# Rotation by DMA exchange, attention's back steps in one group per round, group norm by groups, two tiles in turns behind norms

## The chip, the core and the metric

The kernel runs on one core of one Trainium2 chip: a single program on its five engines, TensorE (PE), VectorE (DVE), ScalarE (ACT), GpSimd (POOL) and SyncE (SP), which work through instruction streams of their own and meet at semaphores. The metric is the device time of one execution in microseconds; the time given is the median of the timed executions.

## What is computed

One layer of a first block on x (512 tokens, width 1024) and a context (256 tokens): a gated feed-forward net (width 2816) on both, a mixing layer (a Fourier part and a two-directional state-space scan with a group norm), and a second feed-forward net. Then two layers of a second block with four branches of 8 heads of 64 channels: A, attention with forget gates; B, attention over 256 chosen tokens; D, attention in a window of 128; C, retention. What the change touches, shortened:

```
def rms_norm(x, g):                         # ahead of and behind every sublayer
    y = x32 * lax.rsqrt(jnp.mean(x32 * x32, axis=-1, keepdims=True) + EPS)
    return (y * g.astype(jnp.float32)).astype(x.dtype)
...
    y = y.reshape(b, L, SSD_WIDTH).astype(x.dtype) * jax.nn.silu(z)
    y = rms_norm(y.reshape(b, L, SSD_GROUPS, SSD_WIDTH // SSD_GROUPS), ...)
    out = jnp.concatenate([fourier_mix(u_f, fourier_w), y], axis=-1) @ w_out
```

In the second block, queries and keys of B, C, D and of the chooser of B are rotated by position (rotary embedding): with a head's 64 channels in two halves of 32, each half is multiplied by a cosine, and the other half by a sine with its sign is added. Attention is then softmax(q k / 8 + mask) v for each head, in fp32.

## The kernel before, in words

Activations lie feature by token: 128 features on the partitions, 512 tokens in the free dimension, eight such tiles for the width of 1024. A weight chunk (128 x up to 1024 elements) is loaded by SP into one of three buffers `raw`, split by ACT into a rounded high part (L1636) and by POOL, rarely by DVE, into the low part (L2538); three matmuls, high x high, high x low, low x high (L1308 to L1310), make one product, here called a triple. A projection tile is eight triples into one PSUM bank. Chunk c+2 is split when chunk c begins, chunk c+5 is loaded then.

The order of everything is a single list of steps, made by `schedule()`: all engines go through the same list, and each emits what it has to do for a step. `Fore` holds the projections of a stage (its "fore" steps), each triple with a cost of 3 x N / 2400 us; `weave` lays "back" steps (the heads) among them: after each fore step it adds cost x rate, and emits one back step whenever a whole one is due. So the back steps are spread evenly, one for each 1/rate us of planned cost. `fm` makes a tile, `lin` several with their evacuation, `tm` tiles with tokens on the partitions, `rope` tiles with a rotation behind them, whose five parts are taken one by one from `tail` after the triples of the next tile.

A rotation: ACT copies the PSUM tile to Q (L1733, event ra); POOL multiplies Q by the cosine (L2565, event rp); DVE multiplies PSUM's four 32-row pieces by the sine into the exchanged rows of the target (L2155, four instructions, event rv, behind which the bank is free), and adds Q (L2162, event rope). There are 22 rotations a layer: qi, ki, kd (2 each), qb, qd, kc, qc (4 each).

Heads A, B and D go through 16 rounds (`PAIRS`: 4 pairs of heads x 4 blocks of 128 queries), with three back steps each. s1: logits on PE for two heads (L1530/L1534, half of the array each, and L1540 for A), maximum with mask on DVE (L2422, L2429), exponential on ACT (L1931). s2, two rounds later: DVE scales by the reciprocal sum (L2439, L2440), PE transposes (L1552), ACT copies (L1945). s3, three rounds later: product with v (L1573), half of the array each. Retention (C) has c1 (L1596, DVE L2481 ff.) and c2 (L1607), and a norm in two steps rn1 and rn2.

The stages of a layer: layer start (qi, ki and a small tile), choosing (A's projections beside 48 rounds of maximum search on DVE), then stage A (qb's four rotations and eight gate tiles, heads A), stage B (qd, kc, vc, first branch; heads B), stage D, stage C, last branch, output, feed-forward net with a convolution. Stage A of layer 0 runs from 1563 us on, of layer 1 from 2721 us.

Behind each norm `prenorm` makes eight pieces: a product on DVE (L2210), a rounded copy on ACT (L1794), the difference on DVE (L2043) or POOL (L2546). The first projection tile waits for the pieces one by one. The state-space part's group norm (gn1 squares on ACT, gn2 sums on PE, gn3 logarithm and exponential on ACT, gn4 products on DVE, gn5 rounding on ACT and difference on DVE) runs in two halves of three tiles, each a whole; the output projection's first three tiles do their triples k = 0 to 4 ahead of the second half and k = 5 to 7 behind it.

## Time and profile before

| | us |
|---|---|
| median of 3 runs | 3737.37 (3733.82 to 3743.4) |
| the profiled execution, whole | 3741.84 |
| its span, first to last instruction | 3740.5 |
| PE busy | 3531.7 |
| DVE, ACT, POOL busy | 1702.6, 1440.1, 1418.1 |
| mean granted clock | 0.97 |

The page gives busy times by engine; a matmul's record is longer than the distance to the next one, since matmuls are pipelined, so the rate is read from the starts. The granted clock is 1.00 at 2.4 GHz and 0.50 at 1.2 GHz. A wait is put down to the instruction that released it. L numbers are lines of the kernel.

### The profile page before, as it was taken

To read this page: it belongs to the slowest core of one execution; us is meant where nothing else is said; L and a number is where in the kernel's file an instruction comes from. 1 tells how busy PE (TensorE), PEld (TensorE's weight loads), DVE (VectorE), ACT (ScalarE), POOL (GpSimd) and SP (SyncE) were. 2 spreads that over 40 slices of the span, in tenths; PEclk is the share of its full clock that TensorE was granted. 3 is DMA by queue.
4 is the path that set the end of the run, shared out by engine and by line. 5 is a ranking of instruction groups with operands and counts; after the bars stand their busy time and mean duration, and the time that the engine had idled before them with its cause. 6 is when DMAs were issued, how large, how long until landed. Compare 5 with 4: busy or idle time off the path is not lost.

```text
span 3740.5 us, 45132 instructions
## 1 busy us (share of the span) xinstructions
PE 3531.7 (94%) x17424; PEld 2777.5 (74%) x17424; DVE 1702.6 (46%) x3129; ACT 1440.1 (38%) x2446; POOL 1418.1 (38%) x651
## 2 busy tenths in 40 slices
PE   6999999998799999999999999999989999999998
PEld 4788889785578877767666778887856766678886
DVE  7876553556410126845542233134755553234143
ACT  3223354554432223344443334342334443334342
POOL 3454433321244444324332444444423332344443
PEclk9999999999999998999999999998999999999999
DMA  7574345221123322212122222323212222223332
GB/s 291 194 248 148 125 158 167 69 91 46 46 91 96 96 88 72 68 51 68 63 79 74 85 79 93 99 91 96 79 46 63 63 68 85 79 79 93 99 95 81
DMA packets 109974, 364.90 MB, mean 98 GB/s; under 512 B 12608, under 2 KB 13504, under 8 KB 109504
## 3 DMA queue, kind: packets, MB, share of 16 engines
q1 hardware_dynamic: 107280, 356.33, 29.4%
q10 hardware_dynamic: 2480, 5.68, 0.5%
q8 instruction: 139, 2.28, 0.3%
q14 instruction: 75, 0.61, 0.1%
HBM read 359.86 MB, written 2.10 MB: 97 GB/s over the span
## 4 chain that ended last, share of the span: by engine, by line
PE 77%; DVE 13%; ACT 5%; issue 2%; DMA 1%; POOL 1%; SPq 0%; DVEq 0%; POOLq 0%; ACTq 0%
PE ps L1308 24%; PE ps L1310 22%; PE ps L1309 22%; PE ps L1552 1%; ACT b L1636 1%; PE ps L1573 1%; DVE b L2174 1%; DVE b L2467 1%; PE ps L1534 1%; DVE b L2466 1%; DVE b L2210 1%; DVE b L2155 1%; POOL b L2538 1%; DVE b L2440 1%; PE ps L1530 1%
## 5 line engine op out<-in xcount | busy, mean ns | idle before, releaser
L2538 POOL TENSOR_TENSOR b<-b,b 128x1024 fp32r<-128x1024 f32 (+2 forms) x579 | 1324.3, 2287 | 2042.0 <-ACT b L1636 2037.0
L1308 PE MATMUL ps<-b,b 128*128 128x512 f32 (+3 forms) x4848 | 1866.2, 385 | 80.1 <-POOL b L2538 23.3
L1309 PE MATMUL ps<-b,b 128*128 128x512 f32 (+3 forms) x4848 | 1804.9, 372 | 0.0
L1310 PE MATMUL ps<-b,b 128*128 128x512 f32 (+3 forms) x4848 | 1804.5, 372 | 0.0
L1308 PEld LDWEIGHTS ps<-b,b 128*128 128x128 f32 x4848 | 934.4, 193 | 348.0 <-issue 139.3
L1310 PEld LDWEIGHTS ps<-b,b 128*128 128x128 f32 x4848 | 934.3, 193 | 161.5
L1309 PEld LDWEIGHTS ps<-b,b 128*128 128x128 f32 x4848 | 936.1, 193 | 145.8 <-issue 4.8
L1636 ACT ACTIVATE b<-b 128x1024 fp32r<-128x1024 f32 (+2 forms) x622 | 607.3, 978 | 261.9 <-PE ps L1310 239.0
L2078 DVE SCALAR_TENSOR_TENSOR b<-ps,b,b 128x511 f32<-128x511 f32 x88 | 66.0, 750 | 371.0 <-ACT b L1687 371.0
L2174 DVE CUSTOM_DVE_ANT_0 b<-b,b,b 128x1024 bf16<-128x1024 f32 x112 | 210.0, 1875 | 20.1 <-DMA b<-in_ada 8.4
L1697 ACT ACTIVATE b<-b 128x512 fp32r<-128x512 f32 (+1 forms) x110 | 64.9, 590 | 390.2 <-DVE b L2087 287.8
L2422 DVE CUSTOM_DVE_ANT_0 b<-ps,b 128x128 f32<-128x128 f32 (+2 forms) x192 | 87.5, 456 | 211.4 <-PE ps L1534 107.0
L2087 DVE TENSOR_TENSOR b<-ps,b 128x512 f32<-128x512 f32 (+1 forms) x66 | 39.6, 600 | 284.8 <-PE ps L1310 284.8
L1931 ACT ACTIVATE b<-b,b 128x128 f32<-128x128 f32 (+2 forms) x192 | 102.5, 534 | 172.9 <-DVE b L2429 131.1
L1767 ACT ACTIVATE b<-b 128x512 f32<-128x512 f32 (+1 forms) x112 | 63.9, 582 | 237.1 <-DVE b L2104 69.8
L2155 DVE TENSOR_TENSOR b<-ps,b 32x512 f32<-32x512 f32 x176 | 120.9, 687 | 68.1 <-ACT b L1733 60.7
L1945 ACT ACTIVATE b<-ps 128x128 f32<-128x128 f32 (+2 forms) x192 | 71.5, 409 | 195.3 <-PE ps L1552 194.1
L2565 POOL TENSOR_TENSOR b<-b,b 128x512 f32<-128x512 f32 x44 | 57.1, 1298 | 189.2 <-ACT b L1733 188.9
L2197 DVE TENSOR_TENSOR b<-b,b 128x512 f32<-128x512 f32 (+1 forms) x77 | 76.7, 996 | 82.3 <-ACT b L1767 81.7
L1687 ACT ACTIVATE b<-ps,b 128x512 f32<-128x512 f32 x88 | 68.6, 779 | 106.7 <-PE ps L1310 106.7
L2093 DVE TENSOR_TENSOR b<-b,b 128x512 fp32r<-128x512 f32 (+1 forms) x110 | 71.1, 646 | 80.2 <-ACT b L1697 80.2
L1552 PE MATMUL ps<-b,b 128*128 128x128 f32 x432 | 72.0, 285 | 30.8 <-DVE b L2440 28.4
(231 smaller groups left out, 2343.8 us busy)
## 6 DMA issues: line engine op xcount, KB each, us to landing
b<-in_w SPq DMA_DIRECT2D x458, 512.0 KB, 3.5
b<-in_ada SPq DMA_DIRECT2D x88, 512.0 KB, 4.7
b<-in_w SPq DMA_DIRECT2D x80, 384.0 KB, 3.1
b<-in_w SPq DMA_DIRECT2D x80, 320.0 KB, 2.9
b<-in_const SPq DMA_DIRECT2D x24, 256.0 KB, 3.8
b<-in_x SPq DMA_DIRECT2D x1, 2048.0 KB, 16.7
out<-b SPq DMA_DIRECT2D x8, 256.0 KB, 2.5
b<-in_c SPq DMA_DIRECT2D x2, 512.0 KB, 10.1
```

What stands on the lines that cost most here:

```text
L1308: pe.matmul(out, a[0], b[0], start=first, stop=False)
L1309: pe.matmul(out, a[0], b[1], start=False, stop=False)
L1310: return pe.matmul(out, a[1], b[0], start=False, stop=last)
L1552: m = pe.transpose(b[:, 128 * i:128 * i + 128], Lg[u % 6][:, 128 * i:128 * i + 128], ident)
L1636: act.activation(whi[j % NS][:, 0:nk * w], raw[j % NR][:, 0:nk * w], ACT.Copy).then_inc(up("hi", j), 1)
L1931: m = act.activation(q[:, 0:hi - lo], q[:, 0:hi - lo], ACT.Exp, bias=sx[:, 1:2], accum_out=sx[:, 2:3])
L1945: act.activation(Pt[u % 4][:, 0:hi - lo], PB[st["bank"][p]][:, 0:hi - lo], ACT.Copy).then_inc(up("pt", a, l, u), 1)
L2155: p = dve.tensor_tensor(dst[o:o + 32, i, :], b[f:f + 32, :], sin[f:f + 32, :], ALU.mult)
L2174: m = dve.tensor_tensor_reduce(spare[:, :], ada_slot(x)[:, :], cb[:, w, :], 1.0, pv("ada_b", p), ALU.mult, ALU.add, mod[:, p, w:w + 1])
L2197: dve.tensor_tensor(Q[6][:, 0:N], Q[6][:, 0:N], n_slot(nid, i)[:, 0:N], ALU.add).then_inc(up("sqa", nid, i), 1)
L2422: dve.tensor_tensor_reduce(Lg[u % 6][:, 0:w], PB[st["bank"][p]][:, 0:w], mk, 0.125, -3e38, ALU.add, ALU.max, sx[:, 0:1]).then_inc(up("t1", ...
L2538: then(pool.tensor_tensor(wlo[j % NS][:, 0:nk * w], raw[j % NR][:, 0:nk * w], whi[j % NS][:, 0:nk * w].bitcast(F32), ALU.subtract), "lop", j)
```

## The change

1. Rotation: behind the copy to Q, ACT issues four DMAs of 32 rows x 2 KB that write Q's halves exchanged into the target; one DVE product with the sine (its sign is turned round in the table) and one sum follow, and POOL's cosine product waits for the DMAs too, since they read Q. The bank is free behind ACT's copy. The two parts come behind the fifth and the seventh triple of the next tile. The waits for the target's last readers move from DVE to ACT.
2. Heads: s3, s2 and s1 of a round are one back step, and DVE's scaling is a step of its own, `sp2`, half a round ahead; c2 and c1 likewise are one. The rates are lower by the same measure, so that the stages still end with their projections. Stage A has its tiles in the order gate, gate, qb.
3. Group norm: each half in two groups of 192 channels with a bank each; the first half's groups come behind yv 1 and 2, the second half's first squares behind yv 4. The triples k = 5 of the first three output tiles are ahead of the last group.
4. `both`: the first two tiles behind a norm (gate and up of each feed-forward net; the two qi tiles at a layer start) take their triples in turns, k by k. The second chunk's "begin", with the split and load that hang on it, comes behind both.

The diff without the event numbering in `number()` (banks of the group norm, free and held marks), the removed names and the PE, ACT and DVE parts of gn2 to gn4, which go by group in the same way:

```diff
         tm("vd", [(w2, l, VD, 128)])
-        cols("qb", w2, l, QB, 512)
+        for m in range(4):
+            cols("gt", w2, l, GT + 256 * m, 256)
+            cols("qb", w2, l, QB + 128 * m, 128)
...
+    def both(self, key, *tiles):
+
+        c = [self.begin(key), self.at[0]]
+        assert self.stream[c[1]][0] == key and self.stream[c[0]][3] == self.stream[c[1]][3] == 8
+        self.at[0] += 1
+        for k in range(8):
+            for t, ch in zip(tiles, c):
+                self.step("mm", t=t, c=ch, q=k, k=k, first=k == 0, last=k == 7, done=k == 7)
+                self.spent(3 * t["N"] / 2400.0)
+        self.step("begin", c=c[1])
+        for t, ch in zip(tiles, c):
+            t["c"] = ch
+        return tiles
...
-    def rope(self, name, count, key, **kw):
-        for m in range(count):
+    def rope(self, name, count, key, at=0, **kw):
+        for m in range(at, at + count):
             t = self.fm(name, m, key, kw["ver"], L, l=kw["l"])
             self.flush()
             self.step("evac", t=t)
-            self.tail = [dict(kind="rope", t=t, part=p) for p in range(5)]
+            self.tail = [None] * 5 + [dict(kind="rope", t=t, part=0), None, dict(kind="rope", t=t, part=1)]
 
     def flush(self):
         while self.tail:
-            self.items.append((self.tail.pop(0), 0.0))
+            step = self.tail.pop(0)
+            if step is not None:
+                self.items.append((step, 0.0))
...
-    out, due, back = [], 0.0, list(back)
+    out, due, back = [], 0.0, [b if isinstance(b, list) else [b] for b in back]
...
-                out.append(back.pop(0))
-    return out + back
+                out += back.pop(0)
+    return out + [s for b in back for s in b]
...
+                if jj == 0:
+                    for t in F.both(key, *[dict(name=x, i=0, N=N, ver=ver, f=f, conv=conv) for x in ("fg", "fu")]):
+                        F.step("evac", t=t)
+                    continue
...
-    def groupnorm(hf):
-        return ([do("gn1", hf=hf, o=o) for o in range(3)] + [do("gn2", hf=hf), do("gn3", hf=hf)]
-                + [do("gn4", hf=hf, o=o) for o in range(3)] + [do("gn5", hf=hf, o=o) for o in range(3)])
+    def groupnorm(hf, o):
+
+        own = (0, 1) if o == 0 else (2,)
+        done = (0,) if o == 0 else (1, 2)
+        return ([do("gn1", hf=hf, o=x) for x in own] + [do("gn2", hf=hf, o=o), do("gn3", hf=hf, o=o)]
+                + [do("gn4", hf=hf, o=x) for x in done] + [do("gn5", hf=hf, o=x) for x in done])
...
-            first = groupnorm(0)
-            B += [do("yv", k=k - 1)] + {3: first[:5], 4: first[5:]}.get(k, [])
+            B += [do("yv", k=k - 1)] + (groupnorm(0, k - 2) if k in (2, 3) else [])
+            if k == 5:
+                B += groupnorm(1, 0)[:2]
...
-    S += weave(F, [do("yv", k=5)] + groupnorm(1), 1.4)
+    for t in tiles:
+        part(F, t, range(5, 6))
+    S += weave(F, groupnorm(1, 0)[2:] + [do("yv", k=5)] + groupnorm(1, 1), 1.1)
     F = fore()
     for m, t in enumerate(tiles):
         if m > 0:
             assert F.begin("wo") == t["c"]
-        part(F, t, range(5, 8))
+        part(F, t, range(6, 8))
...
             for k in range(len(PAIRS) + 3):
-                if k >= 3:
-                    out.append(do("s3", a=kind, l=l, w=k - 3))
                 if 0 <= k - 2 < len(PAIRS):
-                    out.append(do("s2", a=kind, l=l, w=k - 2))
-                if k < len(PAIRS):
-                    out.append(do("s1", a=kind, l=l, w=k))
+                    out.append(do("sp2", a=kind, l=l, w=k - 2))
+                out.append([do(s, a=kind, l=l, w=w) for s, w in (("s3", k - 3), ("s2", k - 2), ("s1", k))
+                            if 0 <= w < len(PAIRS)])
...
-        F.rope("qi", 2, "qi", ver=H, l=l)
+        pair = F.both("qi", *[dict(name="qi", i=m, N=L, ver=H, l=l) for m in range(2)])
+        for t in pair:
+            F.step("evac", t=t)
+        F.tail = [None] * 4 + [dict(kind="rope", t=t, part=p) for t in pair for p in range(2)]
...
-        F.rope("qb", 4, "qb", ver=H, l=l)
-        for m in range(8):
-            t = F.fm("gt", m, "gt", H, L, o=0, l=l)
-            F.step("evac", t=t)
-        S += weave(F, heads("A"), 0.8) + [do("takey", l=l, o=0, t=t) for t in range(4)]
+        for m in range(12):
+            if m % 3 == 2:
+                F.rope("qb", 1, "qb", at=m // 3, ver=H, l=l)
+            else:
+                t = F.fm("gt", m - m // 3, "gt", H, L, o=0, l=l)
+                F.step("evac", t=t)
+        S += weave(F, heads("A"), 0.57) + [do("takey", l=l, o=0, t=t) for t in range(4)]
         F = fore()
         F.rope("qd", 4, "qd", ver=H, l=l)
         F.rope("kc", 4, "kc", ver=H, l=l)
         F.tm("vc", 2, "vc", H, 4, l=l)
         branch(F, 0, 0)
-        S += weave(F, heads("B"), 0.6) + [do("takey", l=l, o=1, t=t) for t in range(4)]
+        S += weave(F, heads("B"), 0.435) + [do("takey", l=l, o=1, t=t) for t in range(4)]
         F = fore()
         F.rope("qc", 4, "qc", ver=H, l=l)
         branch(F, 1, 1)
-        S += weave(F, heads("D"), 0.6) + [do("takey", l=l, o=2, t=t) for t in range(4)]
+        S += weave(F, heads("D"), 0.435) + [do("takey", l=l, o=2, t=t) for t in range(4)]
         F = fore()
         F.lin("gc", 4, "gc", H, L, l=l)
         branch(F, 3, 2)
         B = []
         for k in range(len(PAIRS) + 2):
-            if k >= 2:
-                B.append(do("c2", l=l, w=k - 2))
-            if k < len(PAIRS):
-                B.append(do("c1", l=l, w=k))
+            B.append([do(c, l=l, w=w) for c, w in (("c2", k - 2), ("c1", k)) if 0 <= w < len(PAIRS)])
             if k >= 2 and (k - 2) % 4 == 3:
                 B += [do("rn1", l=l, t=(k - 2) // 4), do("rn2", l=l, t=(k - 2) // 4)]
-        S += weave(F, B, 0.55) + [do("takey", l=l, o=3, t=t) for t in range(4)]
+        S += weave(F, B, 0.35) + [do("takey", l=l, o=3, t=t) for t in range(4)]
...
+                    if name == "qb":
+                        at.wait_ge(*n("sqp", l, 3, 3))
+                    elif name in ("qd", "kc"):
+                        at.wait_ge(*n("s1", "A", l, 31))
+                    elif name == "qc":
+                        at.wait_ge(*n("s1", "B", l, 31))
+                    at.wait_ge(*n("ra", name, l, i))
+                    for o in range(0, 128, 32):
+                        act.dma_start(ropes[name][o:o + 32, i, :], Q[x % 2][o ^ 32:(o ^ 32) + 32, :]).then_inc(s[f"d_half{x % 2}"], 16)
...
-                t, part = st["t"], st["part"]
+                t = st["t"]
                 name, i, l = t["name"], t["i"], t["l"]
-                b, dst = PB[t["bank"]], ropes[name]
-                if part == 0:
+                dst, x = ropes[name], rope_order.index((name, l, i))
+                if st["part"] == 0:
                     at.wait_ge(s["d_cs"], 16 * (l + 1))
-                    at.wait_ge(*n("ra", name, l, i))
-                    if name == "qb":
-                        at.wait_ge(*n("sqp", l, 3, 3))
-                    elif name in ("qd", "kc"):
-                        at.wait_ge(*n("s1", "A", l, 31))
-                    elif name == "qc":
-                        at.wait_ge(*n("s1", "B", l, 31))
-                if part < 4:
-                    o, f = 32 * part, 32 * (part ^ 1)
-                    p = dve.tensor_tensor(dst[o:o + 32, i, :], b[f:f + 32, :], sin[f:f + 32, :], ALU.mult)
-                    if part == 3:
-                        p.then_inc(up("rv", name, l, i), 1)
+                    at.wait_ge(s[f"d_half{x % 2}"], 64 * (x // 2 + 1))
+                    dve.tensor_tensor(dst[:, i, :], dst[:, i, :], sin, ALU.mult).then_inc(up("rv", name, l, i), 1)
                 else:
                     at.wait_ge(*n("rv", name, l, i))
                     at.wait_ge(*n("rp", name, l, i))
-                    q = Q[rope_order.index((name, l, i)) % 2]
-                    dve.tensor_tensor(dst[:, i, :], dst[:, i, :], q[:, :], ALU.add).then_inc(up("rope", name, l, i), 1)
+                    dve.tensor_tensor(dst[:, i, :], dst[:, i, :], Q[x % 2][:, :], ALU.add).then_inc(up("rope", name, l, i), 1)
...
-            elif k == "s2":
+            elif k == "sp2":
...
-            elif k == "evac":
+            elif k == "rope" and st["part"] == 0:
                 t = st["t"]
-                name, i, l = t["name"], t["i"], t.get("l")
-                if name in ROPES:
-                    q = Q[rope_order.index((name, l, i)) % 2]
-                    behind()
-                    at.wait_ge(s["d_cs"], 16 * (l + 1))
-                    at.wait_ge(*n("ra", name, l, i))
-                    then(pool.tensor_tensor(q[:, :], q[:, :], cos, ALU.mult), "rp", name, l, i)
+                name, i, l = t["name"], t["i"], t["l"]
+                x = rope_order.index((name, l, i))
+                behind()
+                at.wait_ge(s["d_cs"], 16 * (l + 1))
+                at.wait_ge(s[f"d_half{x % 2}"], 64 * (x // 2 + 1))
+                then(pool.tensor_tensor(Q[x % 2][:, :], Q[x % 2][:, :], cos, ALU.mult), "rp", name, l, i)
```

## Rows read from the trace of the kernel before

**Rows 1.** The page: busy time by engine, and POOL's cosine product among its groups.
```profile
PE 3531.7 (94%) x17424; PEld 2777.5 (74%) x17424; DVE 1702.6 (46%) x3129; ACT 1440.1 (38%) x2446; POOL 1418.1 (38%) x651
...
L2565 POOL TENSOR_TENSOR b<-b,b 128x512 f32<-128x512 f32 x44 | 57.1, 1298 | 189.2 <-ACT b L1733 188.9
```
**Rows 2.** Windows: us; PE, PEld, DVE, ACT, POOL busy (x count); granted clock; DMA share, GB/s.
```profile
1563.60:1638.00 74.40, 63.15 (x328) 42.61 (x328) 38.17 (x115) 29.44 (x70) 19.20 (x10) 0.91 0.13 43
1638.00:1686.60 48.60, 48.60 (x286) 34.06 (x285) 16.27 (x67) 22.80 (x52) 11.95 (x6) 1.00 0.19 60
...
2198.80:2214.60 15.80, 14.50 (x49) 9.73 (x50) 10.86 (x12) 8.38 (x11) 8.39 (x5) 0.85 0.11 35
...
2250.00:2300.00 50.00, 50.00 (x222) 41.40 (x221) 20.19 (x28) 22.50 (x29) 21.59 (x9) 1.00 0.29 97
```
**Rows 3.** PE's groups by line: busy, mean ns | idle before, with its releasers.
```profile
L1308 PE MATMUL ps<-b,b 128*128 128x512 f32 (+3 forms) x4848 | 1866.2, 385 | 80.1 <-POOL b L2538 23.3 <-DVE b L2043 16.0 <-DVE b L2040 15.2
...
L1552 PE MATMUL ps<-b,b 128*128 128x128 f32 x432 | 72.0, 285 | 30.8 <-DVE b L2440 28.4 <-ACT b L1747 1.8
...
L1350 PE MATMUL ps<-b,b 128*128 128x512 f32 (+1 forms) x70 | 44.6, 763 | 50.9 <-ACT b L1767 33.5 <-DVE b L2197 17.4
L1530 PE MATMUL ps<-b,b 64*128 64x128 f32 (+3 forms) x128 | 27.9, 516 | 6.0 <-DVE b L2155 6.0
L1607 PE MATMUL ps<-b,b 128*64 128x512 f32 (+3 forms) x128 | 25.9, 457 | 5.7 <-DVE b L2484 5.6
```
**Rows 4.** PE's waits in 1563 to 1648, then in 2720 to 2810: total, times, longest.
```profile
PE ps L1552 <- DVE b L2440: 10.3, 4, 3.6
...
PE ps L1552 <- DVE b L2440: 10.2, 5, 3.3
```
**Rows 5.** Timeline of DVE and PE around one stall of stage A: start, us, what.
```profile
1574.95 2.79 DVE L2155 TENSOR_TENSOR b<-ps,b 32x512 f32<-32x512 f32 x4 [1.26 <-ACT b L1733]
...
1578.96 1.21 PE L1552 MATMUL ps<-b,b 128*128 128x128 f32 x4 [3.18 <-DVE b L2440]
```
**Rows 6.** A rotation's products (L2155) and sum (L2162) on DVE: min/median/max ns.
```profile
L2155 DVE TENSOR_TENSOR b<-ps,b x176: 679/686/697, 1427.3 to 3016.8; 32x512 f32<-32x512 f32 x176
...
L2162 DVE TENSOR_TENSOR b<-b,b x44: 685/693/2924, 1430.6 to 3017.6; 128x512 f32<-128x512 f32 x44
```
**Rows 7.** Timeline of PE around single back steps (x4, x6: records of one step).
```profile
1697.85 0.40 PE L1310 MATMUL ps<-b,b 128*128 128x512 f32 x1
1698.18 0.92 PE L1534 MATMUL ps<-b,b 64*128 64x384 f32 x4
1699.03 0.50 PE L1308 MATMUL ps<-b,b 128*128 128x512 f32 x1
...
1711.16 0.82 PE L1552 MATMUL ps<-b,b 128*128 128x128 f32 x6
1711.73 0.47 PE L1308 MATMUL ps<-b,b 128*128 128x512 f32 x1
...
1713.98 0.49 PE L1534 MATMUL ps<-b,b 64*128 64x128 f32 x4
1714.40 0.50 PE L1308 MATMUL ps<-b,b 128*128 128x512 f32 x1
```
**Rows 8.** Four DMAs issued in a row by ACT; issues by size, KB, us to landing.
```profile
639.86 2.46 ACTq L1804 DMA_DIRECT2D b<-in_fw  x4
...
b<-in_w SPq DMA_DIRECT2D x2, 96.0 KB, 2.0
b<-in_const ACTq DMA_DIRECT2D x2, 64.0 KB, 4.0
```
**Rows 9.** Timeline of DVE behind the norm at 2196: products (L2210) between differences.
```profile
2198.53 2.44 DVE L2210 SCALAR_TENSOR_TENSOR b<-b,b,b 128x512 f32<-128x512 f32 x2
...
2201.49 2.43 DVE L2210 SCALAR_TENSOR_TENSOR b<-b,b,b 128x512 f32<-128x512 f32 x2
```
**Rows 10.** PE's waits in 960 to 1010: total, times, longest.
```profile
PE ps L1308 <- DVE b L2370: 6.1, 1, 6.1
```

63 lines of the change are left out of this document (28 added, 35 removed).

## The prediction, written before the changed kernel was run

> **What bounds the kernel now.** I read the page first, then the waits of TensorE (PE), then the windows of stages, and last the timeline around the longest stalls. PE is busy 94% of the span [rows 1], and where it is fed it is full: in a stretch of a feed-forward stage it is busy 50.00 of 50 us with 222 matmuls, 0.225 us each, at the full granted clock of 2.4 GHz [rows 2]. Nothing in the change takes a matmul away. So it can gain only where PE waits, or where the granted clock is at its lower level (1.2 GHz) after such waits. The profiled execution spans 3740.5 us and took 3741.84; the median of the timed runs, 3737.37, is 4.5 below it.
>
> PE idles some 209 us in all (3740.5 - 3531.7). The largest waits [rows 3] are of four kinds. The first, L1350 on L1767 (33.5), sums the squares of a norm, 23.5 of it once at the start of the kernel: not touched. The second, L1308 on L2043 and L2040 (16.0 and 15.2), is the first tile behind a norm, which waits for its input piece by piece. The third, L1552 on L2440 (28.4), is attention's transpose (s2) waiting for VectorE (DVE) to scale the probabilities; beside it stand L1530 on L2155 (6.0) and L1607 on L2484 (5.6). The fourth is group norm, L1308 on L2370, 6.1 in one piece [rows 10].
>
> **Attention, heads A.** Of the 28.4 us, 10.3 lie in the first 85 us of stage A of layer 0 and 10.2 in the same place of layer 1 [rows 4], each with half of L1530's 6.0 and 0.9 on ScalarE (ACT) (L1552 on L1747, 1.8 in all) [rows 3]. The timeline shows the mechanism [rows 5]. At 1574.95 DVE begins four 32-partition products of a rotation, 2.79 us, and only then comes to the scaling of step s2, which waits behind them in program order; PE has by then reached the transposes, and starts them at 1578.96, 3.18 us late. The matmuls behind such a stall run at the lower clock: in 1563.6 to 1638 the mean granted clock is 0.91 and PE is busy 63.15 of 74.40; in the next 48.6 us, without such stalls, the clock is 1.00 and PE is never idle [rows 2].
>
> The change removes this three ways. (a) A rotation costs DVE four products of 687 ns and a sum of 693, 3.4 us; now one product and the sum, each at the sum's 0.69, 1.4 us [rows 6]. (b) The scaling (sp2) stands half a round ahead of the transposes, 1.75 us of the planner's cost, three triples of matmuls at 0.68, so DVE has 2 us more. (c) The four rotations of stage A are no longer at its head: two of three tiles are gates. The sum: 10.3 + 10.2 + 6.0 + 1.8 = 28.3 us of waits. The lower clock: 74.4 x (1 - 0.91) = 6.7 us of full-speed time missing in layer 0, part of it while PE was idle anyway; the six matmuls behind the stall of 1578.96 take 2.70 instead of 1.57, 1.1 us, and there are some four such places, so I take 4 a layer, 8 in all. Of these 36 us I take 31 since DVE can still be late now and then.
>
> **Heads B and D, retention.** The rest of L1552's wait on the scaling is 28.4 - 20.5 = 7.9 us. L1607's 5.6 [rows 3] come at the first c2, which follows its c1 by two back steps (1 / 0.55 = 1.8 us of planned cost each), now by two rounds of 2.9 (1 / 0.35). Of these 13.5 us I take 12.
>
> **One group per round.** Steps s3, s2, s1 no longer have big matmuls between them. What does a break cost? [rows 7]: from a big matmul to the half-array matmuls of s1 it is 0.33 us instead of 0.23 (1697.85 to 1698.18); with 384 columns they hold PE 0.85, with 128 columns 0.42 (1713.98 to 1714.40), so 128 columns are 0.215 of work and 0.2 is left over: a break costs about 0.3. The transposes of s2 use the whole array: six of them hold PE 0.57 us (1711.16 to 1711.73), under 0.1 each, and their break costs nothing that shows: s2 leaves nothing to save. In the merged order the whole-array s2 stands between the two half-array steps, so both keep their entries and exits. The trace shows no half-array step directly ahead of a transpose. Bounds: nothing, and one break of 0.3 saved in each of 96 rounds of heads and 32 of retention (38 us). I take 5, from c2 and c1, which are both half-array: 32 rounds at 0.15.
>
> **The exchange.** The 32-row halves now change places by four DMAs on ACT's queue, which ACT issues itself, behind a wait for its own copy. Four DMAs issued in a row took ACT 2.46 us [rows 8], so each of 44 rotations holds ACT 1.9 to 2.5 us longer; behind them in its queue are the split of the next weight chunk, the copies of transposes and the exponentials. Landing is bounded by the smallest rows, 2.0 us (96 KB on SP) and 4.0 (64 KB on ACT's queue); nearest in queue is the second, nearest in issue-free time the first, I take 3. From the end of the tile: copy 0.6, issue 2, landing 3: 5.6 us. DVE and GpSimd (POOL) come to the rotation five triples later (3.4 us) plus mostly one group (2): 5.4. So DVE waits about nothing to 2 us. POOL's cosine product moves there from the tile's end and waits for the same DMAs, with the low parts of later weight chunks queued behind it, which PE needs two tiles later. DVE's wait delays logits, not the scaling of this round, which has 2 us of slack now: I cost it at nothing, and at 1 us for each of the 32 rotations among rounds at the upper end. If PSUM banks come free earlier, L1530's wait (6.0, counted above) goes.
>
> First the row: the sum at L2162, both inputs in SBUF, takes 693 ns in the median and up to 2924 [rows 6]. The Trainium skill (SBUF - State Buffer, section "SBUF: two separate sides") says why: a DVE operation with two SBUF inputs and a GpSimd operation exclude each other for a whole instruction. The old products had one input in PSUM, the new one has both in SBUF and starts with POOL's cosine product on the same signal. POOL's product at L2565 takes 1298 ns [rows 1]; with that in front DVE's rotation is 0.69 + 1.30 + 0.69 = 2.7 us, not 1.4.
>
> **Two tiles in turns behind norms.** At 2198.8 the first tile starts; its pieces come at DVE's pace, a product and a subtraction in 1.5 us (two of each in 2201.49 - 2198.53) [rows 9], and both first tiles end at 2214.6, with PE at clock 0.85 [rows 2]. In turns, each piece feeds six matmuls (1.36 us at full clock, 2.6 at the lower one). Of 48 matmuls eleven at the lower clock (0.43, 4.7 us) and 37 at 0.2265 end at 2211.9; all at full clock would take 10.9, to 2209.7. Gain 2.7 to 4.9; I take 3 at five places (layer starts, ffn2 and both ffnb), 2 at ffn1. Against it: the split of the chunk after next is issued only behind both tiles, which costs the context's ffn, with its 256 columns, 1, and each layer start, where ACT also issues eight DMAs in a row, 1.5. Together 13.
>
> **Group norm by groups.** PE waits 6.1 us before 967.7, and ACT and DVE do the whole second half in one chain behind the last yv: three squares, two logarithms, two exponentials, then products and roundings. Now its first group is done earlier, and the chain behind yv loses a logarithm, an exponential, a product and a rounding, some 3 us; three triples k=5 come ahead of it. Against it ACT's table may be loaded more often. I take 4; the bounds are 6.1 and, with the first half's norm now earlier among steps that PE waits for, -3.
>
> **Sum.** 31 + 12 + 5 + 13 + 4 = 65 from 3741.8: 3676.8; against the median, which lies 4.5 lower, 3672. I say 3673.
>
> **The rivals.**
> *ACT becomes the bound* (0.15). In the fed part of stage A it is busy 22.80 of 48.60 us [rows 2], 3.9 in a tile of some 8.4, and it waits in order for PE and DVE between copies and exponentials; a rotation adds 2 to 2.5. For it: nothing then goes past a wait in its queue. Against: 2 us are left, and chunks are split two tiles ahead. If each of the 44 rotations costs PE 0.7, 31 is lost: 3704.
> *DVE's product stands behind POOL's* (0.10). Both start on one signal, and DVE's sum of two SBUF tiles has taken 2924 ns before. The rotation is then 2.7 us instead of 1.4, and brings back half of stage A's 31: 3688. The rule of the Trainium skill's SBUF page named above would make this certain; the rows show it in some cases only.
> *Breaks are saved in full* (0.10), the half-array steps keeping pace through the transposes: 3673 - 33 = 3640.
> *Slower* (0.07). The exchange lands late, because ACT sits in exponentials when the tile ends, and DVE stands at the rotation, with the scaling behind it, while PE is at the transposes. That is the old stall with a DMA in place of four products. Its price is that of rows 5, up to 3.2 us and 1.1 of clock. It decides from 65 / 32 = 2.0 us of PE at each rotation among rounds; at 3.5 the time is 3673 + 112 = 3785.
> That it does not do what it says, DVE being late for another reason so that L1552 keeps its waits, gives 3673 + 31 = 3704 and is in the first rival's share.
>
> **Chances.** Forecast 0.58 (own range 3655 to 3695). For 8 in 10 the range takes in the port rule and the larger part of ACT's case, and of the saved breaks: 3645 to 3712. A measurement of this kernel tells 0.3%, 11 us, from no change. Faster 0.92; within 0.02; slower 0.06.
>
> **What would show it.** L1552 on the scaling under 6 us in all; granted clock of stage A above 0.97; L1530's wait for a rotation gone; 96 groups with s3, s2, s1 in a row, as long as the sum of their parts; L1308 behind norms: both first tiles in under 13.5 us; wait before k=5 or 6 of the output projection under 3 us. Wrong would be: DVE idle for the exchange's DMA more than 2 us each and PE's transposes behind it; PE waiting for splits, behind ACT (L1308 on L2538, now 23.3 in all [rows 3], over 35).

## The result, and the profile after

The changed kernel took 3720.56 us (median of 4 runs, 3718.15 to 3724.43), against 3738.69 for the kernel before on the same chip (4 runs, 3733.82 to 3743.4): a ratio of 0.9951, with a 95% interval of 0.9939 to 0.9963. It is faster, by 18 us. Forecast were 3673 (65 less) and a range of 3645 to 3712, so the sign was right, and the size was missed by more than the range allowed for.

The page of the changed kernel, first its engines' line and then groups: line, engine, what it writes and reads, count, busy us, mean ns of one, and idle time ahead with its releaser. The last line is a DMA issue: KB, median us to landing.

```profile
PE 3510.5 (94%) x17424; PEld 2796.0 (75%) x17424; DVE 1672.8 (45%) x2997; ACT 1438.8 (39%) x2448; POOL 1428.4 (38%) x651
...
L2178 DVE TENSOR_TENSOR b<-b,b 128x512 f32<-128x512 f32 x44 | 72.4, 1646 | 98.9 <-DMA b<-b 98.7
L1576 PE MATMUL ps<-b,b 128*128 128x128 f32 x432 | 74.4, 294 | 45.0 <-DVE b L2460 31.2
...
b<-b ACTq DMA_DIRECT2D x176, 64.0 KB, 2.0
```

L1576 is the transpose step s2 (L1552 before). It waited 30.8 us before [rows 3] and waits 45.0 now, 31.2 of it for DVE's scaling (L2460), which the change was to take away. L2178 is the one product that replaces four. It should take 0.69 us and takes 1.65 in the mean, and DVE stood 98.7 us for the exchange ahead of it.

PE's largest waits that differ from [rows 3]: total, times, longest.

```profile
PE ps L1576 <- DVE b L2460: 31.2, 25, 3.1
...
PE ps L1576 <- ACT b L1757: 13.2, 6, 3.5
...
PE ps L1490 <- DVE b L2354: 8.2, 2, 5.2
...
PE ps L1530 <- ACT b L1924: 4.6, 3, 2.2
```

The total hides where that is. These are windows of attention's stages A, B, D and C in layer 0, each from its first triple to that of the next stage, first of the kernel before and then of the changed one (columns as in [rows 2]).

```profile
1559.00:1688.10 129.10, 114.87 (x626) 78.91 (x626) 58.89 (x189) 54.06 (x125) 33.51 (x16) 0.95 0.15 50
1688.10:1820.90 132.80, 130.36 (x786) 96.66 (x785) 74.27 (x211) 61.16 (x137) 48.48 (x24) 1.00 0.20 64
1820.90:1944.30 123.40, 120.76 (x617) 85.48 (x616) 67.88 (x231) 59.02 (x164) 43.67 (x20) 1.00 0.21 69
1944.30:2075.30 131.00, 126.50 (x529) 80.65 (x528) 36.73 (x64) 44.85 (x56) 38.70 (x16) 1.00 0.23 77
```

```profile
1567.00:1677.80 110.80, 107.52 (x626) 77.68 (x625) 46.51 (x169) 52.95 (x124) 33.69 (x15) 0.98 0.21 67
1677.80:1819.00 141.20, 132.95 (x787) 101.47 (x785) 71.19 (x189) 60.64 (x138) 52.44 (x25) 0.96 0.25 77
1819.00:1950.80 131.80, 122.55 (x617) 89.14 (x616) 67.73 (x219) 58.60 (x164) 44.94 (x20) 0.96 0.23 72
1950.80:2073.10 122.30, 122.30 (x529) 81.86 (x528) 36.94 (x64) 44.93 (x56) 38.83 (x16) 1.00 0.24 82
```

Stage A is 18.3 us shorter and C 8.7. But B is 8.4 longer and D 8.4: there PE, which had been at the full clock, 2.4 GHz (granted clock 1.00), now idles 8 to 9 us a stage, and the clock is at its lower level, 1.2 GHz, for a part of it (0.96 in the mean). The same table by the starts of stages for the whole kernel, in us of after minus before:

| stages | after - before | forecast |
|---|---|---|
| A, both layers | -37.6 | -31 |
| B, both layers | +23.3 | part of -12 |
| D, both layers | +16.6 | part of -12 |
| C, both layers | -16.5 | part of -12, and -5 for rounds |
| z and output projection (group norm) | +13.2 | -4 |
| first feed-forward | -6.1 | -2 |
| both feed-forwards at layer ends, both layer starts, ffn2 | -11.2 | -12 |
| context's feed-forward and the step behind it | +2.2 | +1 |

Three rows carry the error: B, D and group norm, a loss of 53 us together. The other rows sum to -69, within a few us of what the forecast gave them or better. All rows together are -16; the profiled execution as a whole is 17 shorter.

A caution on single stages. Kernels that differ from the changed one only elsewhere (the old group norm, no turns, a gate last in stage A, all below) have D at 126.2 to 131.9 us, and the first two of them have B at 140.9 to 145.6, against 141.2 and 147.6. So a difference of up to some 7 us in one B or D of one execution shows nothing by itself. (In the kernel before, whole or with the short low parts tried below, D takes 123.5 or 123.6 us every time.)

B and D don't wait for the same thing. These are PE's waits in B, then in D, of layer 0:

```profile
PE ps L1576 <- ACT b L1757: 6.4, 3, 3.5
PE ps L1576 <- DVE b L2460: 1.4, 3, 0.7
...
PE ps L1576 <- DVE b L2460: 9.2, 8, 2.2
```

D waits for the scaling. B waits first of all for L1757, ACT's copy of a rotated tile out of its PSUM bank (1.8 us in the whole kernel before, 13.2 now, all of it in B); more on this at the fifth experiment. In layer 1 B has 6.8 for the copy and 5.2 for the scaling, D again 9.2.

The timeline of stage D in the changed kernel shows how the scaling comes to be late, here with two rotations in a row. ACTq is the issue of DMAs by ACT; L1660 is ACT's high part of a weight chunk, L2558 POOL's low part of it.

```profile
1846.56 0.58 ACT L1757 ACTIVATE b<-ps 128x512 f32<-128x512 f32 x1
1847.17 2.45 ACTq L1766 DMA_DIRECT2D b<-b  x4
1849.66 1.06 ACT L1660 ACTIVATE b<-b 128x1024 fp32r<-128x1024 f32 x1 [2.52 <-issue]
...
1850.87 2.40 POOL L2558 TENSOR_TENSOR b<-b,b 128x1024 fp32r<-128x1024 f32 x1 [5.17 <-ACT b L1660]
1853.34 1.59 POOL L2584 TENSOR_TENSOR b<-b,b 128x512 f32<-128x512 f32 x1
...
1851.04 2.78 DVE L2178 TENSOR_TENSOR b<-b,b 128x512 f32<-128x512 f32 x1 [1.17 <-DMA b<-b]
1855.04 0.69 DVE L2182 TENSOR_TENSOR b<-b,b 128x512 f32<-128x512 f32 x1 [1.23 <-POOL b L2584]
...
1856.69 2.53 DVE L2460 TENSOR_SCALAR b<-b,b 128x256 f32<-128x256 f32 x1
...
1856.54 0.59 PE L1576 MATMUL ps<-b,b 128*128 128x128 f32 x2 [2.24 <-DVE b L2460]
1859.27 0.69 PE L1576 MATMUL ps<-b,b 128*128 128x128 f32 x2 [2.15 <-DVE b L2460]
...
1853.64 0.66 PE L1597 MATMUL ps<-b,b 128*64 128x128 f32 x8
...
1861.05 0.79 PE L1333 MATMUL ps<-b,b 128*128 128x512 f32 x1
```

ACT copies the tile, issues four DMAs (2.45) and only then computes the high part of the next chunk, so POOL begins the low part at 1850.87. The exchange lands at that very moment, and DVE's product begins at 1851.04, 0.17 us behind POOL. It takes 2.78 us instead of 0.69 and ends 0.55 us behind POOL's instruction. POOL then makes the cosine product, and DVE's sum waits for that. The scaling comes last, and its second row again starts beside a low part of POOL's (2.34 us from 1856.73) and takes 2.53 instead of 0.35. PE reached the group at 1853.64 and left it at 1861.05, 7.4 us later (the last two rows). Of the 44 products of the trace 27 took over 1.3 us, and 22 of those ended within 0.6 us of the end of one of POOL's low parts; so did 9 of the 11 scalings that took over 1.3 us.

### The profile page after: what moved, and what is told of

Read it like the earlier page. It is cut to its first block, busy times and chain, and to the rows that moved or that the text cites. A ratio compares the mean times of both kernels' runs of the same rounds, so it can differ in the third digit from the quotient of the medians.

```text
span 3723.1 us, 45249 instructions
## 1 busy us (share of the span) xinstructions
PE 3510.5 (94%) x17424; PEld 2796.0 (75%) x17424; DVE 1672.8 (45%) x2997; ACT 1438.8 (39%) x2448; POOL 1428.4 (38%) x651
## 4 chain that ended last, share of the span: by engine, by line
PE 76%; DVE 11%; ACT 5%; issue 3%; POOL 2%; DMA 2%; ACTq 1%; SPq 0%; DVEq 0%; POOLq 0%
PE ps L1333 23%; PE ps L1334 22%; PE ps L1335 22%; DVE b L2194 2%; ACT b L1660 2%; PE ps L1576 1%; POOL b L2558 1%; PE ps L1597 1%; ACTq L1766 1%; PE ps L1558 1%; DVE b L2230 1%; PE ps L1631 1%; PE ps L1620 1%; PE ps L1554 1%; DVE b L2460 1%
## 5 line engine op out<-in xcount | busy, mean ns | idle before, releaser
L2558 POOL TENSOR_TENSOR b<-b,b 128x1024 fp32r<-128x1024 f32 (+2 forms) x579 | 1324.3, 2287 | 2183.2 <-ACT b L1660 2166.5
L1333 PE MATMUL ps<-b,b 128*128 128x512 f32 (+3 forms) x4848 | 1842.4, 380 | 75.1 <-POOL b L2558 29.2
L1333 PEld LDWEIGHTS ps<-b,b 128*128 128x128 f32 x4848 | 935.0, 193 | 309.7 <-issue 118.7
L1660 ACT ACTIVATE b<-b 128x1024 fp32r<-128x1024 f32 (+2 forms) x622 | 607.4, 978 | 388.5 <-PE ps L1335 247.4
L2194 DVE CUSTOM_DVE_ANT_0 b<-b,b,b 128x1024 bf16<-128x1024 f32 x112 | 218.7, 1953 | 16.1 <-DMA b<-in_ada 4.1
L2442 DVE CUSTOM_DVE_ANT_0 b<-ps,b 128x128 f32<-128x128 f32 (+2 forms) x192 | 87.3, 455 | 239.0 <-PE ps L1558 136.7
L2178 DVE TENSOR_TENSOR b<-b,b 128x512 f32<-128x512 f32 x44 | 72.4, 1646 | 98.9 <-DMA b<-b 98.7
L1576 PE MATMUL ps<-b,b 128*128 128x128 f32 x432 | 74.4, 294 | 45.0 <-DVE b L2460 31.2
L2460 DVE TENSOR_SCALAR b<-b,b 128x128 f32<-128x128 f32 (+2 forms) x192 | 95.7, 499 | 6.8
```

Source lines behind the costliest of these rows:

```text
L1333: pe.matmul(out, a[0], b[0], start=first, stop=False)
L1576: m = pe.transpose(b[:, 128 * i:128 * i + 128], Lg[u % 6][:, 128 * i:128 * i + 128], ident)
L1660: act.activation(whi[j % NS][:, 0:nk * w], raw[j % NR][:, 0:nk * w], ACT.Copy).then_inc(up("hi", j), 1)
L2178: dve.tensor_tensor(dst[:, i, :], dst[:, i, :], sin, ALU.mult).then_inc(up("rv", name, l, i), 1)
L2194: m = dve.tensor_tensor_reduce(spare[:, :], ada_slot(x)[:, :], cb[:, w, :], 1.0, pv("ada_b", p), ALU.mult, ALU.add, mod[:, p, w:w + 1])
L2442: dve.tensor_tensor_reduce(Lg[u % 6][:, 0:w], PB[st["bank"][p]][:, 0:w], mk, 0.125, -3e38, ALU.add, ALU.max, sx[:, 0:1]).then_inc(up("t1", ...
```

## The experiments

Theory G was that merged rounds make B and D lose (PE comes to three steps at once, and the scaling is late for it), theory R that the rotation's exchange does (DVE stands for the DMAs, ACT for their issue), theory N that group norm by groups costs z and the output projection their 13 us. P is that DVE stands behind POOL's long instruction: first a rival in the experiment with SP's issue, later a theory of its own. The kernel before, measured again beside each set of experiments, took 3741.4 us (the first four), 3741.3 (the next three and the four edits together) and 3740.8 (the rest); ratios are to these. What PE waited for is given in the order total, times, longest.

**The old rotation.** Four products of 32 partitions from PSUM and POOL's cosine product at the tile's end, all else as changed.

```
-  b free behind ACT's copy; 4 DMAs; dst = dst * sin; dst += Q
+  for part in range(4): dst[o:o+32] = b[f:f+32] * sin[f:f+32]   # from PSUM, b held until then
+  dst += Q
```

> The changed kernel with the rotation of before (four 32-row products out of PSUM on DVE, the bank held until the fourth, no exchange by DMA, parts one by one behind the triples); rounds, group norm and turns stay as changed. Against the changed kernel's stages, heads B lost 8.4 and 14.9 us and heads D 8.3 and 8.3 against before. Theory R (the exchange costs ACT 2.45 us of issue for each rotation, lands late, and DVE stands at it with the scaling behind it): B and D come back by 30 to 40 us together, stage A loses at most 8 of its 38, total near 3690. Rival G (the merged rounds make ACT and DVE late by themselves): B and D stay, A loses most of its gain, total 3735 or more.

Measured: 3776.15 us, ratio 1.0092 (1.0076 to 1.0107), 56 us more than the changed kernel. B is 20.7 and 23.6 longer than before, D 17.5 and 17.4. Theory R, as it stood, fell. Rival G had the direction (over 3735), but B and D didn't stay as they were, they got worse by 9 to 12 us each. The waits and one stall say why:

```profile
PE ps L1578 <- DVE b L2179: 59.5, 20, 5.6
```

```profile
1707.03 2.44 DVE L2464 TENSOR_SCALAR b<-b,b 128x256 f32<-128x256 f32 x1
...
1709.96 1.40 DVE L2179 TENSOR_TENSOR b<-ps,b 32x512 f32<-32x512 f32 x2
...
1711.42 0.66 PE L1578 MATMUL ps<-b,b 128*128 128x128 f32 x4 [1.81 <-DVE b L2179]
```

PE's transposes wait for the PSUM bank that the rotated tile holds until its fourth product is done; those products stand behind the scaling on DVE, and the scaling (again 2.44) beside POOL's low part. With the exchange the bank is free behind ACT's copy. Together with the saved DVE time that I had counted, that is worth the 56 us; the two weren't taken apart.

**The old group norm.** Both halves' steps as they were, all else as changed.

```
-  groupnorm(0, 0) at k=2, groupnorm(0, 1) at k=3, groupnorm(1, 0)[:2] at k=5, the rest by groups at 1.1
+  first[:5] at k=3, first[5:] at k=4; [yv 5] + groupnorm(1) at 1.4
```

> The changed kernel with the group norm of before (two halves, each a whole; k = 5 behind the second half). The stages with the Fourier part, the scan and the output projection took 5.1 and 8.1 us more in the changed kernel. Theory N (the first half's groups stand among the scan's steps, where PE waits for them, and the lower clock follows): both come back, 3707. Rival C (it is the clock's accident there, the granted clock was 0.87 against 0.92 in the output projection): they stay within 3 us of the changed kernel, 3718.

Measured: 3704.55 us, 0.9897 (0.9882 to 0.9912). Stage z is back at -1.2 to before (changed: +5.1), the output projection at +0.1 (changed: +8.1). Theory N holds, and for all of the 13 us. That it isn't an accident of the clock shows over all runs: the two stages together take 214.0 to 214.6 us in the eight kernels with group norm by groups and whole low parts there, and 199.7 to 200.8 in the five with the old one.

**SP issues the exchange.** The four DMAs wait and are issued on SP, all else as changed.

```
-  act.dma_start(ropes[name][o:o + 32, i, :], Q[x % 2][o ^ 32:(o ^ 32) + 32, :])
+  sp.dma_start(ropes[name][o:o + 32, i, :], Q[x % 2][o ^ 32:(o ^ 32) + 32, :])
```

> The changed kernel with the four DMAs of each rotation issued by SP instead of ACT, same transfers, same waits. Theory R: ACT is free 2.45 us more in each of 44 rotations, and the exchange lands earlier; DVE's idle time before its product falls from 98.7 us to under 60, heads B and D win 20 to 35 together, total 3690 to 3700. Rival P (what delays DVE is the product itself, 1646 ns in the mean instead of 693, behind POOL's instructions on the port they share): DVE's product stays over 1500 ns, B and D win under 10, total 3712 or more.

Measured: 3695.24 us, 0.9873 (0.9854 to 0.9893), 25 less than the changed kernel, as expected. But not for the reason expected: DVE still stands 93.3 us for the exchange, not under 60, and B and D win 18 us together, not 20 to 35 (A wins the other 10). Rival P missed too, since it had the product stay over 1500 ns. What fell is just the product's own time, and PE's wait on the scaling from 31.2 to 15.6 us.

```profile
L2182 DVE TENSOR_TENSOR b<-b,b 128x512 f32<-128x512 f32 x44 | 31.3, 712 | 93.3 <-DMA b<-b 93.3
```

```profile
1828.88 0.57 ACT L1770 ACTIVATE b<-ps 128x512 f32<-128x512 f32 x1
1829.35 1.05 ACT L1673 ACTIVATE b<-b 128x1024 fp32r<-128x1024 f32 x1
...
1829.47 2.41 SPq L1288 DMA_DIRECT2D b<-b  x4
...
1830.54 2.37 POOL L2562 TENSOR_TENSOR b<-b,b 128x1024 fp32r<-128x1024 f32 x1 [2.51 <-ACT b L1673]
...
1833.29 0.69 DVE L2182 TENSOR_TENSOR b<-b,b 128x512 f32<-128x512 f32 x1 [3.16 <-DMA b<-b]
```

ACT's high part no longer waits for the issue, so POOL's low part runs while the exchange is under way (1830.54 to 1832.91) and is over when the product starts, at 1833.29: 0.69 us. So ACT's issue and POOL's instruction are links of one chain, and theory P took its later form from here. A is at 105.9 in both layers, with PE busy 105.84 of 106.00 us in layer 0. B and D are still 4 to 7 us longer than before.

**The old rounds.** Each back step an item of its own at the old rates, the scaling in one item with its transposes; the exchange stays.

```
-  out.append(sp2(k-2)); out.append([s3(k-3), s2(k-2), s1(k)])      # 0.57, 0.435, 0.435
+  out.append(s3(k-3)); out.append([sp2(k-2), s2(k-2)]); out.append(s1(k))   # 0.8, 0.6, 0.6
```

> The changed kernel with s3, s2 (scaling right ahead of its transposes) and s1 as back steps of their own again, and c2, c1 likewise, at the rates of before; rotation by exchange, group norm and turns stay as changed, and so does the order gate, gate, qb. Theory R: heads B and D do not come back (the late exchange is still there, now without the half round of slack): they stay 8 us or more each above before, stage A keeps two thirds of its 18 us a layer because its rotations are spread; total 3725 to 3745. Rival G: B and D come back to before, total 3690.

Measured: 3809.72 us, 1.0181 (1.0162 to 1.0199), 89 more than the changed kernel; PE waits 84.9 us, 47 times, for the scaling. B is 35.0 and 32.5 longer than before. Theory G fell as well: the exchange without the early scaling is the worst of all. Here the rival that I had called "slower" is seen at work: DVE stands at the rotation, the scaling behind it, PE at the transposes. What theory P says is in it (POOL's 2.39 us begin 0.28 ahead of DVE's product):

```profile
1713.15 2.39 POOL L2563 TENSOR_TENSOR b<-b,b 128x1024 fp32r<-128x1024 f32 x1 [6.91 <-ACT b L1665]
...
1713.43 2.66 DVE L2183 TENSOR_TENSOR b<-b,b 128x512 f32<-128x512 f32 x1
```

So the two parts need each other, and neither alone explains B and D. C, at 131.7 and 133.4, has lost its whole gain: that one comes from the merged steps, not from the exchange.

**Stage A ends with a gate.** The last tile of stage A was a rotated one, with no triples behind it in its stage to cover its exchange.

```
-  gate, gate, rotated (four times)
+  gate, rotated, gate (four times)
```

> The changed kernel, but stage A's tiles run gate, rotated, gate instead of gate, gate, rotated. In the changed kernel the last tile of stage A is a rotated one; its product and sum are put on DVE's list at the end of the stage with no triples in between, ahead of the fetch of the first output and of stage B's first row maxima, so DVE stands until the exchange has landed and PE waits 3.86 us in B's first rounds (at 1689.47, and the same in layer 1), with a clock dip behind it. Theory T (this end tile is a part of B's loss of its own): both stalls are gone, B loses 4 to 6 less in each layer, time 3708 to 3713 against 3720.6. Rival (ACT and the exchange are late at every rotation, and this one only came first): the stall moves to the next round, time 3718 to 3721.

Measured: 3705.85 us, 0.9900 (0.9884 to 0.9916), 15 less than the changed kernel and somewhat more than expected. B is 134.5 and 135.3 (changed: 141.2 and 147.6). In the changed kernel DVE stood 15.17 us ahead of this tile's product, with the fetch of the first output and the row maxima of B's first rounds behind it:

```profile
1682.98 0.69 DVE L2178 TENSOR_TENSOR b<-b,b 128x512 f32<-128x512 f32 x1 [15.17 <-DMA b<-b]
...
1684.92 2.92 DVE L2182 TENSOR_TENSOR b<-b,b 128x512 f32<-128x512 f32 x1 [1.25 <-POOL b L2584]
...
1687.77 2.49 DVE L2525 TENSOR_TENSOR b<-b,b 128x512 fp32r<-128x512 f32 x4
```

PE's first wait in B follows from it. ACT's copy of the next rotated tile stood behind four exponentials, and these behind the row maxima, for which ACT had waited 5.9 us:

```profile
1692.70 0.57 ACT L1757 ACTIVATE b<-ps 128x512 f32<-128x512 f32 x1
...
1693.33 0.69 PE L1576 MATMUL ps<-b,b 128*128 128x128 f32 x2 [3.47 <-ACT b L1757]
```

With the gate last, B waits 2.9 us for the copy in layer 0 and 3.0 in layer 1 (6.4 and 6.8 before this edit). In layer 1 the later stalls of B became smaller too (waits on the scaling 5.2 to 1.8 us), which the estimate had left out. D is as it was (131.9 twice).

**POOL's low part in quarters.** Four instructions of 256 columns instead of one of 1024.

```
-  pool.tensor_tensor(wlo[:, 0:n], raw[:, 0:n], whi[:, 0:n], subtract)
+  for a in range(0, n, n // 4): pool.tensor_tensor(wlo[:, a:a+n//4], raw[...], whi[...], subtract)
```

> The changed kernel, but POOL computes the low part of each weight chunk in four instructions of a quarter instead of one of 1024 columns (2.40 us). Theory P (DVE's short scalings and row maxima, with both operands in SBUF, stand behind the whole of POOL's long instruction; a 128x1 product took 2.33 us beside one): DVE's rows of 2.3 to 2.8 us at the scaling are gone, none over 1.2; PE's wait on the scaling falls from 31.2 to under 15; B and D together lose 12 to 20 less; time 3700 to 3708. Rival X (DVE is late since it waits for the exchange's DMAs, 98.7 us in all): wait on the scaling stays above 24, and POOL's four fixed costs make its list longer, so PE waits more for low parts: 3720 to 3735.

Measured: 3698.32 us, 0.9873 (0.9853 to 0.9894). The product's mean is 976 ns, PE's wait on the scaling 21.5 us (expected under 15), D is +0.5 and +3.6 to before (changed +8.3), B only in layer 1 better; in layer 0 the end tile's stall stays. D's gain is hardly beyond what D does in kernels in which nothing of it was changed (126.2 against 124.0 and 127.1 here), so D's time by itself doesn't decide here; PE's wait on the scaling, 31.2 to 21.5, does speak for P. The low parts keep POOL busy 371 us longer (1695.1 against 1324.3), and PE waits 51.3 us for them instead of 29.2. The context's feed-forward, whose tiles are half as long, pays 12 for it; the stages from there to z get 11 back, 7 of them in z, and why wasn't looked into. Theory P in direction, with a cost that I had put too low.

**POOL's low part of 8 columns.** In the weight chunks of stages A, B, D, C and of the last branch; that leaves out most of the correction product's input there, so it is a test and no kernel to keep.

```
+  e = 8 if STREAM[j][0] in ("gt", "qb", "qd", "kc", "vc", "br", "qc") else n
```

> The changed kernel, but POOL computes only 8 of the 1024 columns of each chunk's low part in attention's stages A, B, D and C and the last branch (this leaves out part of the correction term of these products). It takes POOL's long instruction away beside DVE. Theory P: wait on the scaling under 10 of 31.2, DVE's product of the rotation near 0.7 us in the mean and not 1.6, stages B and D shorter than in the kernel before (132.7 and 123.5): 127 to 131 and 118 to 121; time 3680 to 3692. Rival X: wait on the scaling stays above 20, B above 137, time above 3705.

Measured: 3659.92 us, 0.9778 (0.9763 to 0.9793), 61 less than the changed kernel, more than any theory gave. PE's group of transposes, and windows of B and D in layer 0:

```profile
L1576 PE MATMUL ps<-b,b 128*128 128x128 f32 x432 | 68.8, 285 | 7.2 <-ACT b L1757 5.8 <-DVE b L2460 1.0 <-ACT b L1780 0.3
```

```profile
1672.40:1804.10 131.70, 127.87 (x787) 98.40 (x785) 54.35 (x189) 59.87 (x138) 17.69 (x25) 1.00 0.27 83
1804.10:1922.00 117.90, 117.90 (x618) 87.08 (x617) 54.26 (x219) 58.16 (x164) 15.35 (x20) 1.00 0.25 81
```

The wait on the scaling is 1.0 us instead of 31.2, D of layer 0 has not one idle us (D of layer 1 1.0), both stages have the full clock (0.99 in B of layer 1), and DVE is busy 54 us in each instead of 71 and 68, with the same instructions. DVE still stands 96.7 us for the exchange: that waiting costs PE next to nothing. PE didn't wait for a low part in these stages of the changed kernel, so shorter low parts didn't help it that way. Theory P holds, rival X falls.

**The kernel before, with POOL's low part of 8 columns.** The same cut in the kernel before.

> The kernel before, but POOL computes only 8 of the 1024 columns of each chunk's low part in attention's stages A, B, D and C and the last branch (leaves out part of the correction term). It asks how much the old order lost by POOL's long instruction. Theory P2 (the lock costs the new order far more than the old, since sp2 is one piece of DVE work directly ahead of a whole group): before gains 12 to 22, 3719 to 3729; the new order without the lock, 3659.92, is then 59 to 69 better, which is the 65 of the prediction. Rival (the lock costs both orders alike): before gains some 60, 3675 to 3685, and the change is worth 15 to 25 with or without it.

Measured: 3720.51 us, 0.9944 (0.9930 to 0.9959): 20 us less than before. The new order gains 61 from the same cut. Without POOL's long instruction the change is thus worth 3720.5 - 3659.9 = 60.6 us; with it, 18. By stages, in the profiled executions: A -35, B +4, D -10, C -22 (4 of which the cut had cost the old order), z and output projection +14, the rest -11. B doesn't win even here; its end tile, still there, would explain that.

**The old rotation, with POOL's low part of 8 columns.** The first experiment with the same cut.

> The changed kernel with the rotation of before, and with POOL's low part of only 8 columns in attention's stages (leaves out part of the correction term). With the long one it took 3776.15, PE waiting 59.5 us for banks that a rotation's products hold behind a scaling of 2.4 us. If the lock alone made the old rotation bad with merged rounds: under 3690. If the 2.8 us of products in front of a group are enough by themselves: over 3710, with PE's wait for the products (L1578 on L2179) still above 30.

Measured: 3703.37 us, 0.9897 (0.9881 to 0.9914), PE's wait for the products that hold a bank 29.1 us, down from 59.5. It lies between both expectations: about half of that wait was POOL's, half the products' own. The exchange, with all that goes with it, is worth 3703.4 - 3659.9 = 43 us where POOL doesn't disturb.

**No turns.** All pairs of tiles one after the other again.

```
-  F.both(key, fg0, fu0), F.both("qi", qi0, qi1)
+  F.fm(fg0); F.fm(fu0);  F.rope("qi", 2, ...)
```

> The changed kernel with every pair of tiles one after the other again and the layer's first two rotated tiles as before. By the prediction's term the time is 13 us longer, 3733.5; by the stages of the two traces (ffn1 -6.1, first stage of the layers -3.7 and -0.7, feed-forward at the layers' ends -3.4 and -3.2, ffn2 -0.2, against them the context's ffn +0.8 and dt +1.4) 15 longer, 3736. Rival (these stages were shortened by something else): within 4 of 3720.6.

Measured: 3730.72 us, 0.9972 (0.9962 to 0.9981): the turns are worth 10 us, against 13 forecast. In the profiled executions the stages that have turns or stand behind them are 16 us longer without, and B and D, in which nothing was changed, happen to be 8 shorter; so 13 is borne out by the stages, and the 10 is a net. The first two tiles behind a norm take 13.3 us in turns and 15.8 without at the first layer's end, and 13.1 against 19.2 at the start of the kernel, where I had given 2.

**Four edits together.** SP issues the exchange, the old group norm, a gate last in stage A, no turns in the context's feed-forward.

> The changed kernel with four edits at once: the exchange's four DMAs are issued by SP and not by ACT; the group norm and its place are those of the kernel before; stage A ends with a gate tile; the context's feed-forward stage has no two tiles in turns. If the parts add up: 3720.6 - 25.4 (exchange from SP) - 16.0 (old group norm) - 9 (gate last) - 1 = 3669; range 3664 to 3678. If the gate-last stall and the issue on ACT are one and the same thing, 3676 to 3682.

Measured: 3658.67 us, 0.9777 (0.9763 to 0.9792), 10 better than the expected sum. That sum had 9 for the gate, which measured 14.7; with this the parts give 3663.5, and 5 are left. B is 131.0 and 131.2. That SP's issue and the gate together take away stalls that each alone left in part would explain them, and isn't shown, since D alone varies as much.

**The same, with quarters in attention only.**

> All four edits of the kernel at 3658.67, and POOL's low part in four quarters in attention's stages only, where its list has room (in all stages the quarters cost the context's feed-forward stage 12 us). Theory P: PE's wait on the scaling falls from 15.0 to under 8, stage D of layer 1 comes from 127.0 to under 122, the rest stays: 3642 to 3654. Rival (what is left in D is the exchange's landing, not POOL): 3655 to 3662.

Measured: 3647.36 us, 0.9749 (0.9734 to 0.9763), within what was expected. It is 73 us faster than the changed one and 93 faster than before. Its wait on the scaling:

```profile
PE ps L1588 <- DVE b L2465: 5.2, 7, 0.9
```

## Why the prediction was wrong

*The exchange, "I cost it at nothing".* This is the step that failed, and with it the upper end, "1 us for each of the 32 rotations". What the runs show in place of the nothing, each by one edit: 25 us for the issue on ACT, 15 for the last tile of stage A, 61 for POOL's long instruction. They overlap and don't add up. The landing was on the safe side (2.0 us in the median against 3 taken). DVE stood 98.7 us over 44 rotations, 2.2 each and once 15, where I had "nothing to 2 us"; that was my own sign of being wrong, "more than 2 us each and PE's transposes behind it", and it came. Yet it isn't the standing that costs: with short low parts DVE stands 96.7 us, and PE waits 1.0 for the scaling. I had asked only whether DVE is late for the scaling. I had not asked what the 2.45 us of issue push back on ACT: ACT's high part, and by that POOL's low part, which thereby fell onto the moment of landing. My own text named "the split of the next weight chunk" among what is behind in ACT's queue, and drew the conclusion for PE only, not for POOL and DVE.

*The rival that came true.* It was the second of the text, "DVE's product stands behind POOL's", at 0.10. There I took only POOL's cosine product (1.30 us), half of stage A's gain, 3688. It was the low part, 2.40 us, and it took hold of the scalings too. The Trainium skill (SBUF - State Buffer, section "SBUF: two separate sides") says that a DVE instruction with two SBUF inputs and a GpSimd instruction take the shared ports in turns, each for its whole length, whichever starts first. The traces agree: 0.69 us became 2.78 behind an instruction of 2.40, and became 0.69 again when POOL had ended before. The row that should have warned me stands in the trace of before: scalings at L2440 of up to 2.47 us, 8 of 192 over 1.3 us, and all 8 ended with a low part (within 0.3 us). [rows 6] has such a case, 2924 ns; 6 of the 44 sums took over 1.3 us and ended within 0.6 us of a low part, and I read it as one of a few.

*Heads B and D, "of these 13.5 us I take 12".* The waits went up instead, in D by the same mechanism, in B first of all by the end tile and ACT's late copies. I had looked at what the new place of the rotated tiles does for the head of stage A, not at the end of it: the last one has no triples behind it. Undone, that alone was 15 us. With all edits and the quarters B is at 128.2 and 129.2 us, 4 below before.

*Heads A, 31.* Right: 37.6 less. The granted clock is 0.98 and, with SP's issue, 1.00.

*One group per round, 5.* Too little. Where nothing disturbs, in D of layer 0, PE is busy 117.90 us in the changed order with 8 columns, and 120.85 in the order before with the same cut, a break saving of 3; in C, before and changed, it is 122.3 against 126.5, 4.2. The other layer gives 2.9 and 3.4. B gives less, 130.04 to 127.87 and 129.93 to 129.50. With A, which has no such pair at the full clock, taken as D, that is 6 + 6 + 2.6 + 7.6 = 22 us, an estimate, between the 5 that I took and the 38 of the upper bound. So the whole-array step between two half-array ones doesn't keep all the breaks. In C, idle time of 4.5 us went as well.

*Two tiles in turns, 13.* Right, 10 measured as a net and 16 in its own stages; the start of the kernel brought more, ffn2 (-0.2) nothing.

*Group norm, 4, with a bound of -3 on the bad side.* The second step that failed, by its sign and beyond the bound: 13 lost in its two stages, 16 in time. The wait that it was to shorten is still there, 6.1 us before and 5.9 in two pieces now (L1333 on DVE's L2390). I had named the danger (a norm "among steps that PE waits for") and priced it by nothing. These rows of the changed kernel show one case:

```profile
913.82 0.68 DVE L2371 TENSOR_TENSOR b<-b,ps 128x512 f32<-128x512 f32 x1
...
916.58 0.69 DVE L2377 SCALAR_TENSOR_TENSOR b<-b,b 128x512 f32<-128x512 f32 x1
...
917.31 0.63 ACT L1924 ACTIVATE b<-b 128x512 f32<-128x512 f32 x1 [3.11 <-DVE b L2377]
917.96 1.28 ACT L1927 ACT_TABLE_LOAD   x1
...
917.99 2.08 PE L1530 MATMUL ps<-b,b 128*128 128x512 f32 x2 [2.16 <-ACT b L1924]
...
938.40:952.00 13.60, 9.50 (x32) 6.46 (x34) 10.47 (x13) 5.67 (x15) 2.99 (x1) 0.50 0.13 40
```

The norm's own matmul (L1530) is now placed directly behind the y that it needs. DVE makes that y ready in 3.5 us, ACT squares it, and PE stands; a table is loaded four times instead of two (1.28 us each). Behind the waits of this part the clock stays at 1.2 GHz for 13.6 us (the last row); in the kernel before it is at 2.4 GHz there. That is most of the output projection's loss: its 347 matmuls keep PE busy 73.7 us instead of 68.6, while PE idles only 2 us more. The largest single wait, 5.2 us at L1490 (a broadcast of decays, whose bank DVE's L2354 frees), stands where DVE itself waits for ACT; which of the moved steps puts ACT behind there wasn't taken apart. With the old group norm that line waits 3.1 us in all instead of 8.2, and both stages are back at their old length.

*The test in numbers.* Taken without POOL's long instruction, the change is worth 60.6 us, with group norm's loss of 13 in it. That it comes so near to the forecast 65 is in part luck: group norm is 18 us on the wrong side and B has not gained, and C and the breaks, which I had too low, make up for it. Only A and the turns are near their terms each by itself. What failed beyond the sizes is that the terms were taken for free of one another: the saved waits are only saved while DVE's work isn't stretched.

## What to carry to other kernels

If a change puts a new instruction on an engine's queue, follow what that queue feeds, one link further than the data: here DMA issue delayed ACT, so POOL, so DVE, so PE. Before trusting short DVE work between deadlines, look at the maximum of its group and not at the mean, and see whether the long ones end with a long instruction of POOL's; if so, cut POOL's instruction where POOL has time, or move its start off the moment when DVE must run. And where work is moved by triples of cover, look at the last tile of each stage by itself: behind it there is no cover.
